# Delta rule of a hybrid decoder step: u and y's first half in four quarters of the array, and the sums of y's norm by activations

## The reference

```python
def step(S, inp):
    r_t, w_t, k_t, v_t, kk_t, b_t = inp
    sa = jnp.einsum('bhvk,bhk->bhv', S, kk_t)
    S = S * w_t[:, :, None, :] - sa[..., None] * b_t[:, :, None, :] + v_t[..., None] * k_t[:, :, None, :]
    return S, jnp.einsum('bhvk,bhk->bhv', S, r_t)
...
m = jnp.mean(y, -1, keepdims=True)
var = jnp.mean(jnp.square(y - m), -1, keepdims=True)
y = (y - m) * lax.rsqrt(var + GN_EPS) * gn_g.astype(f32).reshape(H, N) + gn_b.astype(f32).reshape(H, N)
y = y + jnp.sum(rh * kh * r_k.astype(f32), -1, keepdims=True) * vh
out = (y.reshape(B, T, D).astype(x.dtype) * jax.nn.silu(g)) @ w_out
```

## Time and profile before

| | us |
|---|---|
| median of 3 runs | 1451.32 |
| lowest and highest | 1449.02, 1452.41 |
| the profiled execution, its own time | 1445.32 |
| its span, first to last instruction | 1443.5 |
| TensorE busy | 1371.0 |
| VectorE busy | 778.6 |
| ScalarE busy | 614.1 |
| GpSimd busy | 240.5 |

### The profile page before, as it was taken

How to read it: one execution, slowest core, us unless ns; L and a number is a source line. 1 busy time by engine, 2 the same in 40 slices (tenths; PEclk the granted TensorE clock), 3 DMA queues, 4 the chain that set the end, 5 groups by cost and what they waited for, 6 DMA issues and landing times. The chain is left out here.

```text
span 1443.5 us, 32955 instructions
## 1 busy us (share of the span) xinstructions
PE 1371.0 (95%) x13740; PEld 1207.8 (84%) x13740; DVE 778.6 (54%) x1588; ACT 614.1 (43%) x1230; POOL 240.5 (17%) x335
## 2 busy tenths in 40 slices
PE   7999999999999899999999899999999999998997
PEld 7989899887899788888888568899999997665885
DVE  6737344687750157788788543741111213875445
ACT  6725345777851123344334431531111133886224
POOL 0000000000000146677566400000001000213000
PEclk9999999999999979899899999999999999999999
DMA  5723323567778254556564363042324355230202
GB/s 211 222 67 70 98 78 104 142 169 214 220 202 227 64 101 104 116 125 148 133 135 105 96 240 133 1 175 85 90 90 110 90 145 189 87 118 23 89 30 94
DMA packets 265269, 178.43 MB, mean 124 GB/s; under 512 B 169599, under 2 KB 239167, under 8 KB 264207
## 3 DMA queue, kind: packets, MB, share of 16 engines
q1 hardware_dynamic: 233159, 161.37, 39.5%
q10 hardware_dynamic: 31968, 15.04, 3.6%
HBM read 116.21 MB, written 60.46 MB: 122 GB/s over the span
## 5 line engine op out<-in xcount | busy, mean ns | idle before, releaser
L369 PE MATMUL mix_acc<-mix_high,mix_w_high 128*128 128x364 f32 (+1 forms) x768 | 178.6, 341 | 12.4 <-ACT mix_high L435 10.0
L369 PE MATMUL mix_acc<-mix_low,mix_w_high 128*128 128x364 f32 (+1 forms) x768 | 172.2, 333 | 0.6 <-DVE mix_low L589 0.6
L369 PE MATMUL mix_acc<-mix_high,mix_w_low 128*128 128x364 f32 (+1 forms) x768 | 171.1, 332 | 0.0
L369 PEld LDWEIGHTS mix_acc<-mix_high,mix_w_high 128*128 128x128 f32 x768 | 130.4, 190 | 32.1 <-issue 28.4
L369 PEld LDWEIGHTS mix_acc<-mix_low,mix_w_high 128*128 128x128 f32 x768 | 133.4, 190 | 1.2 <-DVE mix_low L589 0.9
L369 PEld LDWEIGHTS mix_acc<-mix_high,mix_w_low 128*128 128x128 f32 x768 | 134.0, 190 | 0.0
L603 DVE TENSOR_TENSOR mix_w_low<-mix_wt,mix_w_high 128x1024 fp32r<-128x1024 f32 x32 | 39.2, 1224 | 127.6 <-ACT mix_w_high L441 127.3
L1612 PE MATMUL out_acc<-qkvg_room_r_high,qkvg_room_w_high 128*128 128x364 f32 (+1 forms) x320 | 105.8, 331 | 1.4 <-DVE qkvg_room_w_low L1964 1.4
L1612 PE MATMUL out_acc<-qkvg_room_r_low,qkvg_room_w_high 128*128 128x364 f32 (+1 forms) x320 | 105.1, 329 | 0.0
L1612 PE MATMUL out_acc<-qkvg_room_r_high,qkvg_room_w_low 128*128 128x364 f32 (+1 forms) x320 | 105.1, 328 | 0.0
L455 ACT ACTIVATE mix_out<-mix_acc 128x364 f32<-128x364 f32 (+1 forms) x96 | 38.3, 472 | 146.0 <-PE mix_acc L369 145.9
(11 more groups left out here) (282 smaller groups left out, 3130.3 us busy)
## 6 DMA issues: line engine op xcount, KB each, us to landing
mix_wt<-in_w_in SPq DMA_DIRECT2D x32, 512.0 KB, 4.6
qkvg_room_wt<-in_w_att SPq DMA_DIRECT2D x20, 512.0 KB, 3.7
delta_bk<-scr_bk SPq DMA_DIRECT2D x68, 128.0 KB, 3.4
delta_kr<-scr_kr SPq DMA_DIRECT2D x17, 512.0 KB, 6.6
scr_kr<-mix_outs SPq DMA_DIRECT2D x16, 512.0 KB, 4.0
scr_bk<-mix_outs SPq DMA_DIRECT2D x16, 512.0 KB, 4.7
early_xpad<-in_xpad SPq DMA_DIRECT2D x8, 548.5 KB, 8.7
scr_xg<-early_xs SPq DMA_DIRECT2D x8, 544.0 KB, 3.0
```

Source lines behind the costliest of these rows:

```text
L369: mm = pe.matmul(acc[:, s, k, 0:width], w[:, s, d, :], r[:, d, n0:n0 + width], start=d == 0 and q == 0, stop=d == DT - 1 and q == 2)
```

## The change

u's products are written to the other half of `chain_bank`'s partitions, so that they use the two off-diagonal quarters, and for each pair y's first two products stand behind them (`make_u_and_begin_y`). `keep_u` reads the flipped halves. On TensorE the second half of the Grams now stands ahead of `end_y`. `sum_y` is new on ScalarE, ahead of keep_lm level 0: eight copies of 128x64 from `wide_bank`, whose accumulators give the sums; `square_y` becomes eight squares whose accumulators give the sums of squares. VectorE's two reductions go.

```diff
-        NORM, SOLVE, TURNED = 6, 15, 6
+        NORM, SOLVE, TURNED = 4, 15, 6
...
-                def make_u(c):
+                def make_u_and_begin_y(c):
+
                     if c < SAMPLE:
                         pe.wait_ge(grown_kept, 6 * c + 6)
                     else:
                         pe.wait_ge(solved_wide, c + 1)
                     pe.wait_ge(z_kept, c + 1)
+                    if c:
+                        pe.wait_ge(normed, NORM * c)
                     for pair in range(DT):
+                        columns = slice(64 * pair, 64 * pair + 64)
+                        for p, half in enumerate(HALVES):
+                            u = pe.matmul(chain_bank[FLIPPED[p], columns], inverse(c, 1)[half, pair, :], z[half, pair, :], start=True, stop=True)
+                        if pair == DT - 1:
+                            u.then_inc(u_made, 1)
                         for half in HALVES:
-                            mm = pe.matmul(chain_bank[half, 64 * pair:64 * pair + 64], inverse(c, 1)[half, pair, :], z[half, pair, :], start=True, stop=True)
-                    mm.then_inc(u_made, 1)
+                            if c < SAMPLE:
+                                y = pe.matmul(wide_bank[half, columns], kr[half, c % 4, 1, pair, :], state[half, c % 2, pair, :], start=pair == 0, stop=False, skip_group_check=True)
+                            else:
+                                y = pe.matmul(wide_bank[half, columns], own_turned[half, pair, 1, :], unit64[half, :], start=pair == 0, stop=False, skip_group_check=True)
+                    y.then_inc(y_begun, 1)
...
                     if live(behind):
-                        make_u(behind)
+                        make_u_and_begin_y(behind)
                     if live(i - 2):
                         turn_y(i - 2)
...
-                    if live(behind):
-                        begin_y(behind)
-                        end_y(behind)
                     if live(front):
                         make_grams(front, 1)
+                    if live(behind):
+                        end_y(behind)
...
                     for p, half in enumerate(HALVES):
-                        act.activation(uv[half, c % 3, :, p, :], src[half], ACT.Copy).then_inc(u_kept, 1)
+                        act.activation(uv[half, c % 3, :, p, :], src[FLIPPED[p]], ACT.Copy).then_inc(u_kept, 1)
                     if c == SAMPLE:
...
-                        act.activation(lower[:], src, ACT.Copy).then_inc(u_plain_kept, 1)
+                        for p, half in enumerate(HALVES):
+                            act.activation(lower[half], src[FLIPPED[p]], ACT.Copy).then_inc(u_plain_kept, 1)
...
+                def sum_y(c):
+                    act.wait_ge(y_made, c + 1)
+                    if c:
+                        act.wait_ge(normed, NORM * c)
+                    for j in range(DT):
+                        act.activation(y2[:, j], wide_bank[:, 64 * j:64 * j + 64], ACT.Copy, accum_out=stat[:, 0, j:j + 1]).then_inc(y_summed, 1)
+
                 def square_y(c):
-                    act.wait_ge(normed, NORM * c + 2)
-                    act.activation(y2[:], wide_bank[:, :].rearrange("p (j n) -> p j n", j=DT), ACT.Square).then_inc(y_squared, 1)
+                    act.wait_ge(y_summed, DT * c + DT)
+                    act.wait_ge(normed, NORM * c + 1)
+                    for j in range(DT):
+                        act.activation(y2[:, j], wide_bank[:, 64 * j:64 * j + 64], ACT.Square, accum_out=stat[:, 1, j:j + 1]).then_inc(y_squared, 1)
 
                 def root(c):
-                    act.wait_ge(normed, NORM * c + 3)
+                    act.wait_ge(y_squared, DT * c + DT)
...
+                    if live(behind):
+                        sum_y(behind)
                     if 0 <= i < SAMPLE:
                         keep_lm(i, 0)
...
                 def centre_y(c):
                     at, y_in = NORM * c, wide_bank[:, :].rearrange("p (j n) -> p j n", j=DT)
-                    dve.wait_ge(y_made, c + 1)
+                    dve.wait_ge(y_summed, DT * c + DT)
                     if c:
                         dve.wait_ge(normed, at)
-                    dve.tensor_reduce(stat[:, 0], y_in, AX, ALU.add).then_inc(normed, 1)
-                    dve.wait_ge(normed, at + 1)
                     dve.scalar_tensor_tensor(y_in, per_head(stat[:, 0]), -1.0 / HD, y_in, ALU.mult, ALU.add).then_inc(normed, 1)
-
-                def sum_squares(c):
-                    at = NORM * c
-                    dve.wait_ge(y_squared, c + 1)
-                    dve.tensor_reduce(stat[:, 1], y2[:], AX, ALU.add).then_inc(normed, 1)
```

More of the change, by code:

```diff
@@ L869, in delta_rule @@
             "bonus_made", "y_made", "normed", "y_squared", "y_rooted", "y_turned", "y_gated"))
-        gained = m.sem("gained")
+        gained, y_summed = m.sem("gained"), m.sem("y_summed")
         own_made, own_kept, own_ended, u_owned, v_owned, own_s, own_done = (m.sem(x) for x in (
@@ L1021, in scale_gain @@
                 def scale_gain(c):
-                    pool.wait_ge(normed, NORM * c + 4)
+                    pool.wait_ge(normed, NORM * c + 2)
                     pool.tensor_tensor(gain[:], gn_g[:], per_head(stat[:, 2]), ALU.mult).then_inc(gained, 1)
@@ L1206, in make_s @@
                     mm.then_inc(s_made, 1)
[L1208 to L1218, removed]
                 def end_y(c):
@@ L1416, in _ @@
                         for b in range(NB):
-                            act.wait_ge(u_plain_kept, 1)
+                            act.wait_ge(u_plain_kept, 2)
                             act.activation(u_own[:, b], lower[:], ACT.Copy, scale=seq_mask[:, b:b + 1]).then_inc(u_owned, 1)
@@ L1446, in _ @@
                 act.wait_ge(bonus_made, 2 * SAMPLE + 2)
-                act.wait_ge(normed, NORM * SAMPLE + 5)
+                act.wait_ge(normed, NORM * SAMPLE + 3)
                 ahead["round_weights"](act)
@@ L1539, in scale_y @@
                     dve.tensor_tensor(y, y, gain[:], ALU.mult).then_inc(normed, 1)
-                    dve.wait_ge(normed, at + 5)
+                    dve.wait_ge(normed, at + 3)
                     dve.wait_ge(bonus_made, 2 * c + 2)
@@ L1578, in _ @@
                         add_own((0, 1))
-                        sum_squares(behind)
                         invert_root(behind)
```

## The result

The changed kernel takes 1432.6 us (median of 4 executions, 1426.3 to 1434.4), the kernel before beside it 1450.2: a ratio of 0.9873, 95% interval 0.9836 to 0.9911. It is faster by 1.3%; the forecast was 1454, 0.2% slower, and the range ended at 1447. The profiled execution took 1431.8 us, its span 1430.0.

The account below looks back on a forecast made before the run. It took a turn as bound by TensorE's 15.7 us plus a 1.18 us hole, VectorE's ring almost as long. Fifteen turns at 0.05 (0.8) plus 1.8 in the last gave 2.6 us more: 1451.3 to 1454, range 1447 to 1470.

Parts of the forecast that it names:

- The ring: Chain of waits across engines from one turn's masks to the next: 16.90 us against 16.85, 0.05 a turn more.
- growing: TensorE's first growing block, released by the kept lower level behind the eight copies: starts 5.84 us after the masks start.
- the two holes named: New TensorE waits: about 1.3 us ahead of growing (copies), 0.7 before the second half of the Grams (masks).
- idle time ahead of the reciprocal: VectorE, its two reductions gone, was to idle about 1 us a turn before the reciprocal.
- the pair on ScalarE: One 128x64 ACTIVATE with its accumulator read: 0.235 us, bounds 0.20 and 0.38; eight are 1.88 us.
- way from the second level to the reciprocal: Ring step from TensorE's second level to VectorE's reciprocal, released by ScalarE's root: 2.38 us, ending at 11.00.
- the forecast's own sign of being wrong: Masks recurring under 16.6 us would mean that a step overlaps which the forecast put in line.
- The last turn: End of the stage: u kept in two parts, eight sums and eight squares make the scaling 1.8 us later.
- the clock: TensorE's granted clock: the forecast sum had no term for it; only rival 2 let it change.
- rival 2: Clock falls more often in the new ring's 2.1 us of holes: three more falls, 13 us, 1467; chance 0.14.
- Rival 3: TensorE's gain comes off the turn because a ring step starts earlier than chained: 9 us less, 1444; chance 0.22.
- Rival 4: Merged block's quarters don't overlap with 64 columns each: 2.18 us, 0.3 a turn, 5 us, 1459; chance 0.06.

Follow-up runs that it names:

- merge_order: Changed kernel with the norm as before (both reductions on VectorE, one square), keeping the merged block and the moved half of the Grams: 1427.1 us.
- merge_only: Kernel before with the merged block alone, second half of the Grams still behind y's end, norm as before: 1449.1 us.
- norm_only: Changed kernel with u and y's order on TensorE as before, so only the norm by ScalarE activations is new: 1427.9 us.
- after_again: The changed kernel itself run again, nothing altered, for its clock in more runs: 1433.1 us.
- before_filled: Kernel before plus one unread 128x448 product on TensorE in the hole ahead of the spreading product: 1433.4 us.
- late_picks: norm_only plus an unread 128x384 product on GpSimd ahead of the picked rows, making the hole at the spreading product again: 1449.3 us.
- squares_only: Changed kernel with y's sum back as a VectorE reduction, sum of squares still by activations: 1428.1 us.
- the three fillings: squares_only, merge_order and the changed kernel with unread products in TensorE's holes: 1430.6, 1429.7 and 1439.4 us.

## Why the prediction was wrong

The ring was right in its order. Step by step from the masks, forecast and measured: Grams 1.34 and 1.44, y's end 2.43 and 2.53, copies 3.63 and 3.73, growing 5.84 and 5.70, second level 8.62 and 8.48, reciprocal 11.00 and 10.72, first solving step 12.14 and 11.87, next masks 16.90 and 16.59. TensorE's gain was spent in the two holes named, VectorE's in 1.09 us of idle time ahead of the reciprocal, as forecast. The parts alone came out as the same ring says (merge_order, merge_only and norm_only: 15.6, 7.3 and 8.5 us at the same clock against 14, 6 and 9).

A term was mis-sized: the pair on ScalarE is 0.20 us, not 0.235, the lower bound given. That is 0.29 of the 0.31 us by which the turn is shorter than forecast; Grams 0.10 later and a faster way from the second level to the reciprocal (2.24, not 2.38) nearly cancel. So the forecast's own sign of being wrong, masks that recur under 16.6 us, came (16.59), without a step that overlaps. The last turn was sized a little too high: from the first masked copy of u to the scaling 11.1 us (804.98 to 816.04) against 10.1 in the earlier trace rows, 1.0 more, and with the 0.6 for u's parts ahead of it 1.6 where 1.8 was forecast. All told the ring gives some 2 us less than before (15 times 0.26, less 1.6); at the same clock it is 4.4 to 5.7. The rest may be before's pauses without a releaser, 3.1 us in its profile.

**The step that failed is the clock.** The forecast held it as it was, and rival 2 let it fall more often, because the new ring has 2.1 us of holes instead of 1.18. It fell less: 0.982 against 0.971, worth 12 of the 17.5 us by the line, and 0.979, worth 9, in the five executions of after_again. The text had itself found that the hole at the spreading product closes, and gave that nothing beyond its length. before_filled shows what that hole costs before: filled, the clock goes from 0.971 to 0.984 and 1.1% comes back. late_picks shows the reverse. That both new holes don't have the same effect at 0.69 and 0.93 us is measured (0.976 to 0.985 in nine executions); why the place matters isn't shown. The Trainium skill ("TensorE: Matmul & The Clock Gate", Part 1) ties the fall to an idle window, and in a second case to frequent micro-idles between groups of products; here the stretches begin beside holes and pauses of 0.3 to 1.2 us in work that otherwise goes on, which is nearer to the second, and a search for long idle times would have missed them.

Rival 3 named the direction and not the cause: what came earlier than chained was the copies (0.29 us, the 0.04 of the pair eight times) and the way from the second level to the reciprocal (0.14), and with the Grams' 0.10 later that is 5 us in 15 turns, not 17.5. Rival 4 is out (1.10 us); so the gotcha on one PSUM bank and different row tiles (the Trainium skill, "TensorEngine Tiling (Array Packing)", Restrictions and Gotchas) costs nothing measurable here, in a block whose kinds both move 64 columns.

**Open.** It isn't known where squares_only and merge_order, with turns of 15.5 and 15.8 us, lose their clock (0.973 and 0.9755). squares_only has next to no hole at the spreading product (two in its profile, 0.9 us in all) and still a lower clock than the change, so that hole isn't the only cause. In the profiles, behind 560 us, its one stretch at 1.2 GHz and one of merge_order's two follow pauses of 0.83 and 1.15 us without a releaser, and merge_order's other one begins at a spreading hole of 0.58; but the timed executions without a profile have no trace. What those pauses are, whether the three fillings lost by them, and why the changed kernel has nearly none, wasn't tried. No version is shown to beat the change beyond its interval. But each part alone gains as much in time as both together (merge_order 0.9852, norm_only 0.9865, the change 0.9873 and 0.9904), and squares_only has the shortest turn; which of them is the fastest isn't settled.

## What to carry to other kernels

Sum the ring of waits (the chain of steps that leads from one turn's masks to the next) from start-to-start rows; here that was right to 0.3 us of 16.6, and with the change's trace at hand to 0.2 for each part. Then price the clock as a term of its own: compare executions at equal granted clock, look which holes and pauses stand ahead of the stretches at 1.2 GHz, and allow for a change that closes or opens such a hole to move the time by more than the hole. One profile can mislead, as before's does; a useless product in the hole is a cheap test. Here it gained 1.1 and 1.2% in the two kernels with a spreading hole of up to 1.2 us, and nothing in three others.

## What the runs showed of the hardware

- Three kernels with a hole of up to 0.9 or 1.2 us at one place of the loop, in an otherwise busy TensorE, have median clocks of 0.964 to 0.971 over the whole execution, while 0.93 us at another place, in every turn, went with 0.976 to 0.985; 2.71 us at that second place gave 0.948. A single such hole mostly passes: in before's trace between 560 and 790 us one of its twelve has a stretch at 1.2 GHz beside it, in merge_only's eight of twelve.
- Three kernels in which the first hole is closed or filled (the norm by activations; one product of filling, in two kernels) have median clocks of 0.982 to 0.984, and opening it again in the first of them gave 0.969.
- An ACTIVATE on 128x64 with a read of its accumulator costs 0.20 us start to start on ScalarE; eight copies took 1.59 us.
- 32 products of 64x64 by 64 columns on all four quarters of the array take 1.10 us, as 16 on two quarters do (1.09).
- TensorE pauses of up to 2.0 us with no releaser came in every other kernel's profile, 0.8 to 8.0 us of them from 560 to 790 us, and nearly not at all in the changed one (0 and 0.9 us in two profiles), where filling its two waits brought 4.6 us. merge_order waits twice a turn too and has 3.8 us of them. What brings them isn't shown.
